# Hybrid attention and trunk layers on one core: last products of the hybrid layers in three passes, GpSimd scaling the probabilities, modulations moved into the norms

## What is computed

```python
# hybrid layer (SEQ = 256), heads_n: 512 features of branch n after attention, times its gate
merged = sum(sigmoid_gate[n] * (heads_n @ w_branch[n]) for n in range(3))   # 3 x (512 -> 1024)
x = x + merged @ w_out                                                      # 1024 -> 1024
# trunk layer
y = rms_norm(x) * (1 + scale) + shift          # adaLN: shift, scale, gate from silu(c) @ mod_w
p = exp(s - max(s)); p = p / sum(p); o = p @ v # attention, 8 and more heads
```

## Time and profile before

| | us |
|---|---|
| median of 3 runs | 2627.74 (2626.24 to 2631.07) |
| profiled execution, its own time | 2630.32 |
| its span | 2628.5 |
| PE busy | 2530.1 (96%) |
| DVE busy | 1287.5 (49%) |
| ACT busy | 939.2 (36%) |
| POOL busy | 85.6 (3%) |
| mean granted clock of TensorE | 0.987 |

### The profile page before, as it was taken

How to read it: one execution, slowest core, us unless ns; L and a number is a source line. 1 busy time by engine, 2 the same in 40 slices (tenths; PEclk the granted TensorE clock), 3 DMA queues, 4 the chain that set the end, 5 groups by cost and what they waited for, 6 DMA issues and landing times.

```text
span 2628.5 us, 39007 instructions
## 1 busy us (share of the span) xinstructions
PE 2530.1 (96%) x16138; PEld 2110.1 (80%) x16138; DVE 1287.5 (49%) x1946; ACT 939.2 (36%) x1434; POOL 85.6 (3%) x97
## 2 busy tenths in 40 slices
PE   7999998999999999999998999999999999988999
PEld 6998888998878888876556788887888887856999
DVE  4567535477444433345675433343443333366654
ACT  4346414346243212242254422222421224355532
POOL 0000000000000000002820000000000000000000
PEclk9999999999999999999999999999999999999999
DMA  5447544446442322322451323223323232542453
GB/s 215 168 148 254 177 145 167 160 171 213 150 161 91 103 89 90 123 81 89 170 224 40 137 78 122 89 95 120 106 88 105 93 108 76 182 166 105 171 196 107
DMA packets 62687, 353.07 MB, mean 134 GB/s; under 512 B 14400, under 2 KB 17601, under 8 KB 26433
## 3 DMA queue, kind: packets, MB, share of 16 engines
q1 hardware_dynamic: 62528, 350.82, 37.9%
HBM read 349.75 MB, written 1.05 MB: 133 GB/s over the span
## 4 chain that ended last, share of the span: by engine, by line
PE 90%; DVE 6%; ACT 2%; issue 1%; DMA 1%; SPq 0%; ACTq 0%; DVEq 0%
PE psum L1162 16%; PE psum L1163 16%; PE psum L1164 16%; PE psum L742 16%; PE psum L779 6%; PE psum L781 6%; PE psum L780 6%; DVE slab L2200 2%; PE psum L835 1%; PE psum L841 1%; PE psum L836 1%; DVE stat L2148 1%; PE psum L805 1%; PE psum L1051 1%; PE psum L806 1%
## 5 line engine op out<-in xcount | busy, mean ns | idle before, releaser
L1162 PE MATMUL psum<-h_hi,w_hi 128*128 128x512 f32 (+1 forms) x1408 | 515.7, 366 | 13.4 <-DVE h_lo L2052 11.8
L1164 PE MATMUL psum<-h_hi,w_lo 128*128 128x512 f32 (+1 forms) x1408 | 514.1, 365 | 0.0
L1163 PE MATMUL psum<-h_lo,w_hi 128*128 128x512 f32 (+1 forms) x1408 | 514.0, 365 | 0.0
L2214 DVE TENSOR_TENSOR w_lo<-wring,w_hi 128x1024 fp32r<-128x1024 f32 (+1 forms) x240 | 318.6, 1330 | 308.8 <-ACT w_hi L1693 308.3
L1693 ACT ACTIVATE w_hi<-wring 128x1024 fp32r<-128x1024 f32 (+1 forms) x240 | 273.2, 1142 | 524.5 <-PE psum L1164 518.1
L779 PE MATMUL psum<-h_hi,w_hi 128*128 128x256 f32 (+1 forms) x1176 | 358.5, 305 | 9.0 <-DVE ring_lo L2077 8.2
L781 PE MATMUL psum<-h_hi,ring_lo 128*128 128x256 f32 (+1 forms) x1176 | 349.3, 297 | 0.0
L780 PE MATMUL psum<-h_lo,w_hi 128*128 128x256 f32 (+1 forms) x1176 | 348.9, 297 | 0.0
L2077 DVE TENSOR_TENSOR ring_lo<-wring,w_hi 128x1024 fp32r<-128x1024 f32 x192 | 227.6, 1223 | 184.2 <-ACT w_hi L1572 182.5
L1162 PEld LDWEIGHTS psum<-h_hi,w_hi 128*128 128x128 f32 x1408 | 268.6, 191 | 56.9 <-issue 12.7
L1163 PEld LDWEIGHTS psum<-h_lo,w_hi 128*128 128x128 f32 x1408 | 268.8, 191 | 41.6
(11 more groups left out here) (172 smaller groups left out, 2981.5 us busy)
## 6 DMA issues: line engine op xcount, KB each, us to landing
wring<-in_w_b_ffn_in SPq DMA_DIRECT2D x84, 1024.0 KB, 4.9
wring<-in_w_mod SPq DMA_DIRECT2D x72, 1024.0 KB, 5.0
wring<-in_w_b_ffn_out SPq DMA_DIRECT2D x64, 704.0 KB, 4.0
wring<-in_w_b_merge SPq DMA_DIRECT2D x24, 1024.0 KB, 4.8
wring<-in_w_b_out SPq DMA_DIRECT2D x16, 1024.0 KB, 4.9
wring<-in_w_b_in SPq DMA_DIRECT2D x16, 1024.0 KB, 5.9
wring<-in_w_b_q SPq DMA_DIRECT2D x12, 1024.0 KB, 4.8
wring<-in_w_b_k SPq DMA_DIRECT2D x12, 1024.0 KB, 4.9
```

What stands on the lines that cost most here:

```text
L1162: nc.tensor.matmul(acc, wh[:, k, :], rhs_hi[k], start=(k == 0), stop=False)
L1163: nc.tensor.matmul(acc, wh[:, k, :], rhs_lo[k], start=False, stop=False)
L1164: return nc.tensor.matmul(acc, wl[:, k, :], rhs_hi[k], start=False, stop=(k == n - 1))
L2214: V.tensor_tensor(part_piece(w_lo, q, i), raw_piece(c, i), part_piece(w_hi, q, i).bitcast(F32), ALU.subtract).then_inc(weights_split, 1)
```

## The change

1. The branch and output products of b1.0 and b1.1 are made in three passes. DVE writes each head pair raw, rounded and rest; ACT rounds the merged sums (`round_merged`), DVE takes their rest. The weights are rounded and split like the others: branch chunks 0 and 1 in steps 12 and 13 of attention, the others while the products run. In ACT's order the rounding of chunk 13 of the fillers stands ahead of `copy_rows`, and `context_squares` stands behind the rounding of the second `out` chunk.
2. In b2.0 and b2.1 GpSimd scales the probabilities; DVE keeps the reciprocal.
3. Seven modulations move: b1.1's attention gives five, b2.1's heads and attention one each; each of the trunk's norms takes one more, b2.1.n1 two more. `EARLY_MODS` sets how many stand ahead of the last sum and ahead of `rs`.
4. For products on 256 tokens the first four pieces go in the order `FIRST_SHORT`: k below 4 of all four, then piece after piece. b1.1's plan has its modulations on both sides of the two q chunks.
5. The last chunk of b2.1's projections (nv) is loaded after two of the heads' modulations, and split inside the heads' scaling. In the index stage the splits go at even steps.

```diff
-MOD_PLACES = [("b1.0.att", 12), ("b1.1", 2), ("b1.1.att", 9), ("b2.0.n1", 2), ("b2.0.nm", 3), ("b2.0.conv", 3), ("b2.0.uq", 7),
-              ("b2.0.heads", 6), ("b2.0.att", 7), ("b2.0.n2", 2), ("b2.1.n1", 3), ("b2.1.nm", 3), ("b2.1.heads", 6), ("b2.1.att", 5),
-              ("b2.1.n2", 2)]
+MOD_PLACES = [("b1.0.att", 12), ("b1.1", 2), ("b1.1.att", 4), ("b2.0.n1", 3), ("b2.0.nm", 4), ("b2.0.conv", 3), ("b2.0.uq", 7),
+              ("b2.0.heads", 6), ("b2.0.att", 7), ("b2.0.n2", 3), ("b2.1.n1", 5), ("b2.1.nm", 4), ("b2.1.heads", 5), ("b2.1.att", 4),
+              ("b2.1.n2", 3)]
...
+FIRST_SHORT = [(k, i) for k, i in FIRST if k < KH_X] + [(k, i) for i in range(PARTS) for k in range(KH_X, KD)]
+
+EARLY_MODS = {"b1.1": (0, 1), "b2.0.n1": (1, 2), "b2.0.nm": (1, 3), "b2.0.n2": (1, 2), "b2.1.n1": (1, 3), "b2.1.nm": (1, 3), "b2.1.n2": (1, 2)}
...
-        for c in range(1, 12):
+        for c in range(1, 14):
             out[c].append(("split", l, c))
...
-                    for m, _ in MODS["b1.1"]:
-                        plan.extend([("b1.1.q0", 1, KD * 256), (f"mod{m}", 1, KD * 256)])
+                    first, second = [(f"mod{m}", 1, KD * 256) for m, _ in MODS["b1.1"]]
+                    plan.extend([first, ("b1.1.q0", 2, KD * 256), second])
...
-            plan += [("b2.1.in", 8, KD * 256)]
-            mods("b2.1.heads")
-            plan += [("b2.1.in", 1, KD * 256)]
+            between = [(f"mod{m}", 1, KD * 256) for m, _ in MODS["b2.1.heads"]]
+            plan += [("b2.1.in", 7, KD * 256)] + between[0:2] + [("b2.1.in", 1, KD * 256)] + between[2:]
...
+            def branch_features(nm, c, rhs):
+
+                for i in range(2):
...
+                    for t in range(2):
+                        out, cols = acc[:, SEQ * t:SEQ * t + SEQ], slice(P * t, P * t + P)
+                        for k, (r_hi, r_lo, ready) in enumerate(rhs):
...
+                            nc.tensor.matmul(out, hi[:, k, cols], r_hi, start=(k == 0), stop=False)
+                            nc.tensor.matmul(out, hi[:, k, cols], r_lo, start=False, stop=False)
+                            mm = nc.tensor.matmul(out, lo[:, k, cols], r_hi, start=False, stop=(k == KW - 1))
...
-                norm_sums(nm, range(summed_before, KD))
+                early, middle = EARLY_MODS.get(nm, (0, 0))
+                norm_sums(nm, range(summed_before, KD - 1))
+                hold(nm)
+                norm_mods(nm, 0, early)
+                norm_sums(nm, range(KD - 1, KD))
+                norm_mods(nm, early, middle)
...
-                        features(f"{nm}.y{n}{j}", c, w, 512, [(oT[n][:, k, :], f"{nm}.att.o{4 * n + k}") for k in range(KW)],
-                                 SEQ, 4)
+                        branch_features(f"{nm}.y{n}{j}", c, [(heads_hi(n, k), heads_lo[n][:, k, :], f"{nm}.att.o{4 * n + k}")
+                                                             for k in range(KW)])
...
-                    features(f"{nm}.out{j}", c, w, 256, [(merged[:, k, :], f"{nm}.mg{k // 2}") for k in range(KD)], SEQ, 2)
+                    sums = [(merged_hi[k // KW][:, k % KW, :], merged_lo[:, k, :], f"{nm}.ml{k // 2}") for k in range(KD)]
+                    if j == 0:
+                        paired_features(f"{nm}.out0", c, sums)
+                    else:
+                        features3(f"{nm}.out{j}", c, sums, SEQ, 2)
...
-            context_squares()
+                last = last_chunks(l)
+
+                def round_merged(n):
+                    if E.new(f"{nm}.mg{n}"):
+                        act.wait_ge(*E.at(f"{nm}.mg{n}"))
+                    A(merged_hi[n // 2][:, 2 * (n % 2):2 * (n % 2) + 2, :], merged[:, 2 * n:2 * n + 2, :], ACT.Copy).then_inc(copied, 1)
+                    act.wait_ge(copied, E.step(copied, f"{nm}.mh{n}"))
+
+                for m in range(2, 6):
+                    round_chunk(last[m])
+                for i in range(2):
+                    round_piece(last[6], i)
+                    round_merged(i)
+                round_piece(last[7], 0)
+                round_merged(2)
+                round_merged(3)
+                round_piece(last[7], 1)
+                if l == 1:
+                    context_squares()
+                for m in range(8, 10):
+                    round_chunk(last[m])
...
+            def normalise(nm):
+
+                probs = PROBS[nm][0]
+                for v, u in enumerate(ATT[nm]):
+                    if E.new(f"{nm}.inverse{v}"):
+                        pool.wait_ge(*E.at(f"{nm}.inverse{v}"))
...
+                            nc.gpsimd.tensor_scalar(pv, pv, st[:, at:at + 1], 1.0, ALU.mult, ALU.mult).then_inc(normalised, 1)
...
+                            if n < 2 or k < KW:
+                                split_piece(last_chunks(l)[2 * n + j + 2], i)
+                            if n == 2:
+                                if k == KD - 2:
+                                    split_piece(last_chunks(l)[7], 0)
+                                if E.new(f"{nm}.mh{k // 2}"):
+                                    dve.wait_ge(*E.at(f"{nm}.mh{k // 2}"))
+                                V.tensor_tensor(merged_lo[:, k:k + 2, :], mg, merged_hi[k // KW][:, k % KW:k % KW + 2, :].bitcast(F32),
+                                                ALU.subtract).then_inc(combined, 1)
...
+                if i == 3:
+                    split_chunk(projections[8])
                 if i == 4:
                     rope_pieces("b2.1.heads")
-            split_chunk(projections[8])
```

More of the change, by code:

```diff
@@ L177, in split_stage @@
     return ".ffn" in s or s in ("b2.0.in", "b2.0.out", "b2.1.in", "b2.1.out") or s[0:3] == "b1." and s[5:] in (
-        "merge",) + tuple(f"{part}{br}" for part in "qkvg" for br in range(3))
+        "merge", "branch", "out") + tuple(f"{part}{br}" for part in "qkvg" for br in range(3))
 LOOPED = {s: (n % SLOTS, n // SLOTS) for s, n, _ in weight_plan() if "_in" in s}
@@ L399, in program @@
         vv = [s1.take(QT, WIDTH) for _ in range(3)]
-        gg = [s1.take(KW, SEQ, area=i // 2) for i in range(3)]
+        gates_at = []
+        gg = []
+        for i in range(3):
+            gates_at.append(s1.at[i // 2])
+            gg.append(s1.take(KW, SEQ, area=i // 2))
         probs_at = s1.at[1]
@@ L409, in program, with rounded, heads_hi @@
         oT = gg
+        def rounded(name, at, *shape):
+            return nc.alloc_sbuf_tensor_at(name, [P] + list(shape), F32R, offset=slab_at + 4 * at)
+        keys_at = AREAS[0][0] + 3 * KW * SEQ
+        heads_lo = [rounded(f"heads_lo{i}", at, KW, SEQ) for i, at in enumerate(gates_at)]
+        heads_hi2 = rounded("heads_hi2", keys_at + KW * SEQ, KW, SEQ)
+        merged_lo = rounded("merged_lo", values_at, KD, SEQ)
+        merged_hi = [rounded("merged_hi0", values_at + KD * SEQ, KW, SEQ), rounded("merged_hi1", keys_at + 2 * KW * SEQ, KW, SEQ)]
+        def heads_hi(br, pair):
+            return heads_hi2[:, pair, :] if br == 2 else h_hi[:, 4 * br + pair, SEQ:TOK]
         isc = s1.take(CAUSAL, area=1)
@@ L813, in first_features, with paired_features @@
                         E.step(piece_multiplied, names[i // per] if i % per == per - 1 else None)
+            def paired_features(nm, c, rhs):
+                acc = take(f"{nm}.0")
+                q, lo = piece_of[c], mixer_lo(c)
+                pe.wait_ge(weights_split, q + 2)
+                for k, t in [(k, t) for ks in (range(KD - 2), range(KD - 2, KD)) for t in range(2) for k in ks]:
+                    r_hi, r_lo, ready = rhs[k]
+                    if E.new(ready):
+                        pe.wait_ge(*E.at(ready))
+                    out, last = acc[:, SEQ * t:SEQ * t + SEQ], k == KD - 1
+                    nc.tensor.matmul(out, mixer_hi(q + t)[:, k, :], r_hi, start=(k == 0 and t == 0), stop=False)
+                    nc.tensor.matmul(out, mixer_hi(q + t)[:, k, :], r_lo, start=False, stop=False)
+                    mm = nc.tensor.matmul(out, lo[:, k, P * t:P * t + P], r_hi, start=False, stop=(last and t == 1))
+                    if last:
+                        if t:
+                            E.name_next(f"w{c}")
+                        mm.then_inc(piece_multiplied, 1)
+                        E.step(piece_multiplied, f"{nm}.0" if t else None)
             def tokens3(nm, c, lhs, halves, toks, first=0, close=True):
@@ L909, in norm, with hold, norm_mods @@
                 E.step(summed, f"{nm}.rs")
+                norm_mods(nm, middle, None)
+            def hold(nm):
                 if nm == "b1.1":
+                    state["held"] = [state["c"] + 1, state["c"] + 2]
+                if nm in ("b2.0.nm", "b2.1.nm"):
+                    state["held"] = [state["c"] + 3]
+                if nm.replace(".n", ".ffn") in FFNS:
                     state["c"] += 1
[L912 to L913 removed]
+            def norm_mods(nm, a, b):
+                after = nm.replace(".n", ".ffn")
+                bank = piece_number(after, 0) if after in FFNS else state["bank"]
```

(7 more changed lines are left out.)

104 lines of the change are left out of this document (73 added, 31 removed).

## The result

The changed kernel takes 2585.64 us (median of 4 runs, 2582.8 to 2587.89), the kernel before beside it 2626.99 us. The ratio is 0.9833, 95% interval 0.9822 to 0.9845: 1.67% faster, against 2584 us forecast. The quotient of the two medians is 0.9843, 41.4 us, and lies inside that interval. The profiled execution has a span of 2583.5 us at a mean granted clock of 0.992 (before 0.987).

What follows compares the result with a forecast made beforehand. PE, busy for 96% of the span, was taken as the bound. Gains and losses summed to 44.2 us off the profiled 2630.3 us, 2586.1; with the median 2.6 us lower, the forecast was 2584 us, own range 2576 to 2592.

Steps and rivals of the forecast that it cites:

- Three passes, +26.0: Branch and out products of b1.0 and b1.1: 13.0 us less per layer, if ACT and DVE keep up.
- The squares, -7.9: b1.1 behind the branch products: PE newly stalls 6.3 us for the context's squares, plus 1.6 us of lowered clock.
- four squares: 14.5 us: b1.1, ACT: the four squares end 14.5 us after PE finished the first n = 2 piece; PE wants them at 8.5.
- The turning, -4.0: End of both hybrid attentions (b1.0, b1.1): two roundings ahead of the `mod_rows` copy cost PE 2.0 us each.
- First projections, +7.5, +1.5: b1.1: the k chunk's 5.91 us wait and 1.6 us of clock go; b1.0: most of 2.3 us of waits goes.
- ffn on 256 tokens, +1.5: The ffn on 256 tokens: PE's 1.6 us wait for `w_lo` goes, a gain of 1.5 us.
- The nv chunk, +5.1: b2.1's nv product: PE's 3.54 us wait goes (+3.5), and the clock need not fall (+1.6).
- the load is one modulation earlier too: b2.1's nv chunk: besides earlier splits, its load comes one modulation earlier, as part of the 3.5 us gain.
- Modulations, +6.5: Modulations moved into the trunk's norms: 6 x 1.07 less 1.3 gives +5.0 us, and a kept clock +1.5.
- GpSimd, +8.5: Both trunk attentions: scaling on GpSimd relieves DVE, which sets the pace; gain 8.5 us, between 0 and 15.
- rival of a GpSimd that brings nothing: Trunk attentions: contention and the semaphore hop eat DVE's gain, the 8.5 us go; 2594 us, chance 0.13.
- Index stage, 0: Index stage of b1.0 and b1.1: splits at even steps were put down at nothing.

Runs made afterwards that it cites:

- experiment 5: Changed kernel with one plain fp32 matmul in place of the three passes in the branch products alone, rounding and subtracting kept: 2604.21 us, ratio 0.9898 to the kernel before.
- experiment 1: Changed kernel with the context's first four squares put back right behind b1.1's attention on ACT: 2579.94 us, ratio 0.9812 to the kernel before.
- experiment 2: Changed kernel with the chunk of attention step 13 in b1.0 and b1.1 rounded and split in step 14: 2582.91 us, ratio 0.9819 to the kernel before.
- experiment 9: Kernel before with only the order FIRST_SHORT for the first pieces on 256 tokens, b1.1's plan unchanged: 2624.3 us, ratio 0.998.
- experiment 7: Changed kernel with five of the seven moved modulations back in b1.1's attention: 2594.71 us, ratio 0.9873 to the kernel before.
- experiment 3: Changed kernel with DVE scaling the probabilities again in both trunk attentions, nothing on GpSimd there: 2594.73 us, ratio 0.9867 to the kernel before.
- experiment 8: Kernel before with one line changed, index-stage splits in b1.0 and b1.1 behind even steps, not odd ones: 2623.86 us, ratio 0.9987.

## Why the prediction came out right, point by point

The time (2584 against 2585.64 us) is better than its terms. That it is so close is luck: several terms were off, and they cancel.

- **Three passes, +26.0:** right. Branch products of b1.0 with the out products gained 12.3 us (I had 13.0 - 0.5), and taking the branch part back costs 7.9 and 7.1 us at like clock (experiment 5), where my price gives 7.7 for each. There is no wait for merged_lo in b1.0. The 12.3 us need a full clock: three executions with the same code there took 67.3 and not 64.7 us.
- **The squares, -7.9:** right in kind, oversized in the wait: 4.35 us, not 6.3. The step that failed is "four squares: 14.5 us". PE sums each square as it comes, which is 1.3 us earlier, and a DVE piece of n = 2 took 3.19 and not 3.38 us. Nor is it DVE's lag, as my count from DVE's delays suggested; experiment 5 shows a chain behind the last product. The clock's part is larger than I had: 0.51 over 703 to 710 us, 3.1 us and not 1.6. So 4.35 + 3.1 = 7.5 us, and 7.3 us in experiment 1, come near the 7.9 because two errors cancel.
- **The turning, -4.0:** right in the wait, 2 x 1.83 us. The half clock behind b1.1's turning comes on top, 1.7 us (experiment 2), which I had only as a bound.
- **First projections, +7.5, +1.5:** right in size, but I had the order freeing 2.8 us; it frees 1.4 (experiment 9). Of the ffn on 256 tokens, +1.5, nothing came: PE waits 1.77 us for w_lo there still.
- **The nv chunk, +5.1:** its own 3.54 us went, but the step "the load is one modulation earlier too" failed. The plan has the load behind two of the heads' modulations where it stood behind six, and the step left out what a chunk that waits in the ring does to the loads behind it. PE waits 1.95, 3.78 and 0.39 us for modulations; the heads' stage got 2.5 us longer with one modulation fewer. I asked what is late next for b1.1's plan, and not here.
- **Modulations, +6.5:** right in kind. Five of the seven are worth 5.4 us at their place and cost nearly nothing in the norms (experiment 7), where I had taken off 1.3 us. Whether they also keep the clock is open: the whole of experiment 7 is 8.7 to 10.5 us, but 2.6 us of it stand where nothing was changed.
- **GpSimd, +8.5:** right, 8.9 us (experiment 3). A pass of 512 columns takes 697 ns on the mean, as the fastest, 691 ns, in the earlier trace rows; DVE's work in these steps reads PSUM for the most part (28 of 46.6 us in b2.0, 34 of 41.3 us in b2.1). At the end of b2.0's attention, of the four passes of 256 columns in a unit the two beside DVE's L2481 and L2486 (two SBUF inputs) take 0.90 and 0.79 us and the others 0.48 to 0.52. That agrees with the Trainium skill (GPSIMD Engine Reference, Key points: contention with VectorE when it has two SBUF inputs). The longest pass of 512 columns, 971 ns, was not traced to one of these. The rival of a GpSimd that brings nothing is out.
- **Index stage, 0:** missed. The even steps gave 3.4 us (experiment 8). I had not looked at PE's waits marked "issue" (1.64 us in each layer), which stood behind DVE's splits.

So the sum of terms missed some 3.4 us in the index stage, and had some 9 us too much for nv and w_lo: for nv a wait of 3.54 us went and 6.1 us came, against +5.1, and w_lo gave nothing of +1.5. What makes up for it lies in the clock and in pieces of the other terms; it was not taken apart further.

## What to carry to other kernels

A chunk that is loaded early into a ring of slots holds its slot until it is used: count which load waits for it, four places on, before moving it. When an in-order engine takes over work, look at what small item stands behind it in that queue (here four squares of 0.44 us and one copy of 0.4 us) and put that first. Work that hangs on nothing belongs where PE waits for a chain; there it is worth its own time.
